# Two accumulator halves of each output: one reduction on VectorE in place of a ScalarE copy and a VectorE add

## The chip, the cores and the metric

The kernel runs on one core of one Trainium2 chip. The metric is the device time of one execution in microseconds (us).

## The reference, cut to what matters

The program is a two-block network on one sequence of T = 256 rows of width D = 2048, all in fp32. The first block has an even layer (gated short convolution, a state-space mixer `ssd` with 4 groups, memory attention) and an odd layer (latent attention `mla` with 16 heads, memory attention); the second has a retention mixer (8 heads) and a squared-ReLU MLP of width 8192. What matters here is that nearly all of the work is matrix products of the 256 rows with weights that are used once:

```python
proj = h @ w_in                                   # 2048 -> some 9000 columns, even layer
q  = (rms_norm(c_q,  mla_q_norm_w)  @ mla_w_uq)   # odd layer, rank 768
kv = (rms_norm(c_kv, mla_kv_norm_w) @ mla_w_ukv)  # odd layer, rank 512
return x + jnp.concatenate([y_a, y_b, y_m], axis=-1) @ w_out
...
def squared_relu_mlp(h, w_up, w_down):
    return jnp.square(jax.nn.relu(h @ w_up)) @ w_down
```

and that each product's result is then scaled, gated, added to the residual, or fed to an attention.

## The kernel before, in words

**Products in three parts.** fp32 factors are split in two parts each, hi and lo, of the type that TensorE takes at its full rate (`F32R`): w = w_hi + w_lo, h = h_hi + h_lo. A product is w_hi·h_hi + w_hi·h_lo + w_lo·h_hi. The activations lie transposed, as tiles of 128 features by T = 256 positions, hi and lo side by side (`hs`, `ys`, `lat`: 512 columns). A "panel" is the weights of 128 output features: 16 tiles of 128x128 as a rule, 6 or 8 in parts of the mla stage. For each tile, line 1821 multiplies w_hi with the 512 columns [h_hi, h_lo] into one accumulator bank of 512 columns, and line 1827 multiplies w_lo with the 256 columns of h_hi into the bank's first 256 columns. So at the end the bank `pj[:, k]` holds the output in two halves, columns 0 to 255 and 256 to 511, and the output is their sum. There are two such banks (`NB = 2`), used in turn.

**Panels by rows.** The value projections and the MLP's down projection are computed the other way round (`row_panel`, lines 1851 to 1855): all three parts go to the same 512 columns, and nothing is left to add. The change does not touch how these are taken from the bank.

**Splitting the weights.** The weights arrive by SyncE's queue in `raw` (4 panels deep). For each half of a panel, ScalarE writes `w_hi` (a copy that rounds, line 508), and VectorE writes `w_lo = raw - w_hi` (line 947). `w_hi` and `w_lo` hold two panels, so the split of panel p + 2 waits until TensorE has begun to use the half behind it in panel p (`half_started`), and TensorE waits for `split_ready`, VectorE's last word on a half.

**Taking an output.** `copy_half` on ScalarE (lines 510 to 513) waits for `output_ready` from TensorE and copies the bank's first half to the buffer `half`; `evac` on VectorE (lines 949 to 960) waits for `half_copied`, adds the bank's second half to `half`, and signals `evacuated`. With `scale` it then multiplies the sum by a row of factors (line 960). TensorE opens output o + 2 in the same bank only after output o is evacuated. 371 outputs go this way.

**The order of the work.** Each engine's program is written out by hand. In one panel step the engines do, with smaller pieces of the stage between:

```python
split(name, i, j, 0)        # ScalarE: w_hi of the first half of panel j + 2
copy_half(name, i, j)       # ScalarE
split(name, i, j, 1)
...
split(name, i, j, 0)        # VectorE: w_lo of the same halves
evac(name, i, j, dst)       # VectorE
split(name, i, j, 1)
```

ScalarE's second split of a step has no wait of its own for the buffer: it relies on the wait for `output_ready` that stands ahead of it.

**The two places to follow.** In the mla stage (8 passes, `mla_body`, 8 panel steps each) steps 0 to 2 make two query outputs and the rotary one (output 2), step 3 makes outputs 3 and 4 from one panel: output 4 takes the bank that output 2 had. Output 2 goes to `qr`, which GpSimd turns (line 469) before VectorE adds the turned part (lines 1564 and 1566) and TensorE multiplies for the scores (line 2173). In the ssd stage (4 passes, `ssd_body`, 12 panels of 16 tiles each) the last two steps hold the state-space tail: VectorE's lines 1338 to 1342, then 1325 to 1333 (the sum of squares), one small product on TensorE at tile 15 of panel 11 (line 2076), the variance (line 984), ScalarE's rsqrt by Ln and Exp (lines 523 to 527, with a load of the activation table), then output 11, VectorE's Newton step (lines 971 to 977), the gated memory output and the scaled outputs (line 1358 and 1363). The stage out0 behind it starts from those.

Of the kernel before, what the change touches and what calls it, by code (L numbers as in the profile page):

```python
# [25 lines left out]
P = 128  # L26
T = 256
# [95 lines left out]
def build(nc, streams, w_dt, vecs, consts, mla_mask, ret_tab, ret_decay, pos, x, mem, out):  # L123
    ctx = ExitStack()
    with ctx:
# [14 lines left out]
        kv = sb("kv", [P, 2048])  # L140
        half = sb("half", [P, NB, T])
        wdt = sb("wdt", [P, 16, 32])
# [88 lines left out]
        output_ready = sem("output_ready")  # L231
        half_copied = sem("half_copied")
        evacuated = sem("evacuated")
# [261 lines left out]
        def _(act):  # L495
# [13 lines left out]

            def copy_half(name, i, o, weight=1):  # L510
                c = outputs(name, i)
                act.wait_ge(output_ready, c(o, 1))
                A(half[:, c.slot(o, NB)], pj[:, c.slot(o, NB), 0:T], ACT.Copy).then_inc(half_copied, weight)  # L513

            def rows_out(name, i, r, dst, scale=1.0, sums=None):
                O = outputs(name, i)
                act.wait_ge(output_ready, O(4 + r, 1))
                A(dst, pj[:, O.slot(4 + r, NB)], ACT.Copy, scale=scale, accum_out=sums).then_inc(half_copied, 1)
                act.drain().then_inc(evacuated, 1)
# [43 lines left out]
            def mem_body(i):  # L563
                for j in range(8):
                    split("mem", i, j, 0)
                    if j < 4:
                        copy_half("mem", i, j)
                    if j == 7:
# [27 lines left out]
            def gate_body(i):  # L596
                for j in range(4):
                    if j == 1:
                        act.wait_ge(evacuated, outputs("gate", i)(0, 1 + NB))
                        A(th_g, z_g, ACT.Tanh, scale=0.5).then_inc(S["gate_tanh"], 1)  # L600
                    split("gate", i, j, 0)
                    copy_half("gate", i, j)
                    split("gate", i, j, 1)
# [6 lines left out]
            def gate_out_body(i):  # L610
                for j in range(4):
                    if i == 1 and j == 2:
                        act.wait_ge(S["dte_logits"], 1)
                        A(cum_out, mx[0:64, 2, 0:128], ACT.Copy).then_inc(S["cum_ready"], 1)
                        A(cum, mx[:, 1, 64:128], ACT.Copy)
                        A(dte, mx[:, 1, 0:32], ACT.Exp).then_inc(S["dte_ready"], 1)
                    copy_half("gate_out", i, 2 * j)
# [6 lines left out]
                    copy_half("gate_out", i, 2 * j + 1)  # L624
                    split("gate_out", i, j, 1)
# [3 lines left out]
            def residual(name, ppo):  # L629
# [3 lines left out]
                def body(i):  # L633
                    for j in range(len(SHAPES[name][0])):
                        split(name, i, j, 0)
                        if j % ppo == ppo - 1:
                            o = j // ppo
                            copy_half(name, i, o)
                        split(name, i, j, 1)
# [25 lines left out]
            def ssd_body(i):  # L665
                O = outputs("ssd", i)
                M = Count(0, 1, i)
                for j in range(12):
# [66 lines left out]
            def latent_q():  # L735
                for j in range(6):
# [6 lines left out]
                    if j == 0:  # L743
                        rsqrt(NORM["b_latent"] + 1, nv, ny)
                    copy_half("latent_q", 0, j)
                    split("latent_q", 0, j, 1)
# [6 lines left out]
            def latent_kv():  # L753
                for j in range(5):
                    if j == 4:
                        lat_squares(4, kvsq, 0, 4)
                    split("latent_kv", 0, j, 0)
                    if j == 1:
                        mem_turned(0)
                    copy_half("latent_kv", 0, j)  # L760
# [14 lines left out]
            def memq_body(i):  # L775
                name = f"memq{i}"
                M = Count(4, 2, i)
                for j in range(4):
# [12 lines left out]
                    copy_half(name, 0, j)  # L791
                    split(name, 0, j, 1)
# [14 lines left out]
            def mla_body(i, opening=False):  # L807
                O = outputs("mla", i)
                for j in range(8):
# [11 lines left out]
                    if j == 3:  # L821
                        copy_half("mla", i, 3)
                    split("mla", i, j, 0)
                    if j == 3:
                        copy_half("mla", i, 4)
                    if j < 3:
                        copy_half("mla", i, j)
                    if j == 4:
                        act.wait_ge(output_ready, O(5, 1))
                        A(vrow_, pj[:, O.slot(5, NB)], ACT.Copy).then_inc(half_copied, 1)  # L830
                        act.drain().then_inc(evacuated, 1)
                    if j == 5:
                        copy_half("mla", i, 6)
                    if j == 7:
                        act.wait_ge(S["mla_pt"], i * 1 + 1)
                        A(pt_.rearrange("p (u c) -> p u c", u=2), mx[:, 3:5, 0:384],
                          ACT.Copy).then_inc(S["mla_pt_copied"], 1)
                        copy_half("mla", i, 7)
                    split("mla", i, j, 1)
# [6 lines left out]
            def ret_body(name, first):  # L846
                def body(i, opening=False):
                    O = outputs(name, i)
                    for j in range(12):
# [16 lines left out]
                        if j < 4 or j >= 8:  # L866
                            copy_half(name, i, j if j < 4 else j - 2)
                        if j == 7:
# [18 lines left out]
            for b in range(FF_BLOCKS):  # L887
                def up_body(i, opening=False):
                    for j in range(4):
                        split(f"up{b}", i, j, 0)  # L890
                        copy_half(f"up{b}", i, j)
                        split(f"up{b}", i, j, 1)
# [6 lines left out]
                def down_body(i):  # L899
                    name = f"down{b}"  # L900
                    for j in range(4):
# [3 lines left out]
                        if j == 3:  # L905
                            act.wait_ge(output_ready, outputs(name, i)(1, 1))
                            act.nop().then_inc(half_copied, 2)
                        split(name, i, j, 1)
# [27 lines left out]
        def _(dve):  # L936
# [671 lines left out]
            def ret_body(name, first):  # L1608
                def body(i, opening=False):
# [30 lines left out]
                    for j in range(12):  # L1640
# [817 lines left out]
```

## Time and profile before

| | |
|---|---|
| median of 3 runs | 2695.31 us (2694.66 to 2696.9) |
| the profiled execution | 2695.13 us, span of its instructions 2693.6 us |
| TensorE products (PE) | busy 2659.9 us, 99% of the span |
| TensorE weight loads (PEld) | 2291.9 us, 85% |
| VectorE (DVE) | 1889.4 us, 70% |
| ScalarE (ACT) | 1395.7 us, 52% |
| GpSimd (POOL) | 61.4 us, 2% |
| transfers | 502.20 MB, 186 GB/s |
| granted TensorE clock | full in every slice but the last |

The profile is of one execution. A group's row gives the line, the engine, what is written from what, the count, the busy time, the mean of one in ns, and behind the last bar the idle time of that engine just ahead of these instructions with what ended it. PE rows tell of multiplications, PEld rows of weight loads, which run ahead of them. Ends of multiplications are modelled, so a gap in PE is best read from starts.

### The profile page before, as it was taken

Reading aid. Unit: us, or ns where it says so; the run is one execution under the profiler, and the core shown is the slowest. Engines: PE = TensorE matmul, PEld = TensorE weight load, DVE = VectorE, ACT = ScalarE, POOL = GpSimd, SP = SyncE. Lnnn points to the kernel's source line nnn. Section 1 sums busy time; section 2 is a strip of 40 time slices with the busy share of each in tenths; the row PEclk is TensorE's granted clock in tenths of the full one; section 3 lists DMA queues with packets and bytes.
Section 4 is the critical chain, followed back from the end, with each engine's and each line's share of the span. In section 5 each row is a group of like instructions: output and inputs, shape, how many; then the busy total and the mean of one; then the engine's idle time right before and its main releaser. Section 6 shows DMA issues by size and latency. Waiting matters only on the chain.

```text
span 2693.6 us, 42729 instructions
## 1 busy us (share of the span) xinstructions
PE 2659.9 (99%) x14622; PEld 2291.9 (85%) x14622; DVE 1889.4 (70%) x2945; ACT 1395.7 (52%) x2090; POOL 61.4 (2%) x84
## 2 busy tenths in 40 slices
PE   8999999999999999999999999999999999999998
PEld 7888888888888888888888888888888888888886
DVE  6766678888777777776777656666776576575674
ACT  5554467665555555565555545554554343444443
POOL 0000000000000111000000000000000000000000
PEclk9999999999999999999999999999999999999999
DMA  7755565555673454666555555555555656556553
GB/s 272 208 202 187 187 209 191 180 186 174 193 245 129 151 156 141 201 194 211 177 186 177 176 189 173 181 179 173 201 178 198 198 186 193 189 187 199 190 187 125
DMA packets 120007, 502.20 MB, mean 186 GB/s; under 512 B 9168, under 2 KB 9296, under 8 KB 82160
## 3 DMA queue, kind: packets, MB, share of 16 engines
q1 hardware_dynamic: 115456, 480.28, 53.4%
q0 software_dynamic: 4032, 20.03, 2.2%
q8 instruction: 54, 0.88, 0.1%
q10 hardware_dynamic: 432, 0.74, 0.1%
q14 instruction: 33, 0.27, 0.0%
HBM read 492.58 MB, written 8.43 MB: 186 GB/s over the span
## 4 chain that ended last, share of the span: by engine, by line
PE 85%; issue 7%; DVE 3%; ACT 2%; DVEq 1%; POOL 1%; DMA 0%; ACTq 0%; SPq 0%; POOLq 0%
PE pj L1821 39%; PE pj L1827 19%; PE pj L1851 7%; PE pj L1855 7%; PE pj L1854 7%; DVE w_lo L947 1%; ACT w_hi L508 1%; POOL gen L469 1%; PE pj L2279 1%; PE mx L1869 1%; PE mx L2237 1%; PE pj L2004 1%; PE pj L2282 0%; PE mx L2255 0%; DMA xT<-in_mem 0%
## 5 line engine op out<-in xcount | busy, mean ns | idle before, releaser
L947 DVE TENSOR_TENSOR w_lo<-raw,w_hi 128x1024 fp32r<-128x1024 f32 (+1 forms) x1010 | 1130.6, 1126 | 487.8 <-ACT w_hi L508 477.4
L508 ACT ACTIVATE w_hi<-raw 128x1024 fp32r<-128x1024 f32 (+1 forms) x1010 | 981.8, 977 | 719.7 <-PE pj L1821 377.8
L1821 PE MATMUL pj<-hs,w_hi 128*128 128x512 f32 x3792 | 1205.9, 399 | 0.6 <-DVE w_lo L947 0.6
L1827 PEld LDWEIGHTS pj<-hs,w_lo 128*128 128x128 f32 x3792 | 712.3, 188 | 167.9
L1827 PE MATMUL pj<-hs,w_lo 128*128 128x256 f32 x3792 | 745.8, 278 | 0.0
L1821 PEld LDWEIGHTS pj<-hs,w_hi 128*128 128x128 f32 x3792 | 581.4, 189 | 5.9 <-issue 1.9
L1821 PE MATMUL pj<-ys,w_hi 128*128 128x512 f32 x1328 | 418.2, 396 | 5.4 <-DVE ys L967 3.8
L513 ACT ACTIVATE half<-pj 128x256 f32<-128x256 f32 x371 | 140.8, 379 | 385.7 <-PE pj L1827 364.5
L1827 PEld LDWEIGHTS pj<-ys,w_lo 128*128 128x128 f32 x1328 | 249.5, 188 | 58.8
L1827 PE MATMUL pj<-ys,w_lo 128*128 128x256 f32 x1328 | 261.1, 278 | 0.0
L1851 PE MATMUL pj<-w_hi,ys 128*128 128x512 f32 x576 | 224.6, 390 | 0.0
L1854 PE MATMUL pj<-w_lo,ys 128*128 128x512 f32 x576 | 224.2, 389 | 0.0
L1855 PE MATMUL pj<-w_hi,ys 128*128 128x512 f32 x576 | 224.1, 389 | 0.0
L1821 PEld LDWEIGHTS pj<-ys,w_hi 128*128 128x128 f32 x1328 | 202.4, 189 | 7.3 <-DVE ys L967 4.4
L955 DVE TENSOR_TENSOR gen<-pj,half 128x256 f32<-128x256 f32 x228 | 95.8, 420 | 61.5 <-ACT half L513 59.8
L1855 PEld LDWEIGHTS pj<-w_hi,ys 128*128 128x128 f32 x576 | 108.1, 188 | 22.5
L1851 PEld LDWEIGHTS pj<-w_hi,ys 128*128 128x128 f32 x576 | 108.1, 188 | 22.3
L1854 PEld LDWEIGHTS pj<-w_lo,ys 128*128 128x128 f32 x576 | 108.2, 188 | 22.2
L1851 PE MATMUL pj<-w_hi,hs 128*128 128x512 f32 x256 | 100.5, 393 | 0.0
L1855 PE MATMUL pj<-w_hi,hs 128*128 128x512 f32 x256 | 99.7, 390 | 0.0
L1854 PE MATMUL pj<-w_lo,hs 128*128 128x512 f32 x256 | 99.7, 390 | 0.0
L1821 PE MATMUL pj<-lat,w_hi 128*128 128x512 f32 x208 | 68.7, 407 | 2.6 <-DVE gen L960 1.5
(346 smaller groups left out, 2002.4 us busy)
## 6 DMA issues: line engine op xcount, KB each, us to landing
raw<-in_w_up SPq DMA_DIRECT2D x64, 1024.0 KB, 4.9
raw<-in_w_down SPq DMA_DIRECT2D x64, 1024.0 KB, 5.7
raw<-in_w_ssd SPq DMA_DIRECT2D x48, 1024.0 KB, 4.8
raw<-in_w_ret_a SPq DMA_DIRECT2D x48, 1024.0 KB, 4.8
raw<-in_w_ret_b SPq DMA_DIRECT2D x48, 1024.0 KB, 4.9
raw<-in_w_out SPq DMA_DIRECT2D x64, 640.0 KB, 3.9
raw<-in_w_gate SPq DMA_DIRECT2D x32, 1024.0 KB, 4.9
raw<-in_w_mem SPq DMA_DIRECT2D x16, 1024.0 KB, 7.3
```

The lines of the kernel that those rows point to most:

```text
L469: ins = nc.gpsimd.tensor_tensor(qro[a:a + 32], qr[b:b + 32], sinT[b:b + 32], ALU.mult)
L508: A(hi, w, ACT.Copy).then_inc(hi_ready, 1)
L513: A(half[:, c.slot(o, NB)], pj[:, c.slot(o, NB), 0:T], ACT.Copy).then_inc(half_copied, weight)
L947: TT(lo, w, hi.bitcast(F32), ALU.subtract).then_inc(split_ready, 1)
L955: TT(dst, pj[:, k, T:2 * T], half[:, k], ALU.add).then_inc(evacuated, weight)
L1821: ins = mm(pj[:, k], w_hi[:, s + g, u], moving[t], start=opens and t == 0, stop=False)
L1827: ins = mm(pj[:, k, 0:T], w_lo[:, s + g, u], moving[t][:, 0], start=False, stop=closes and t == order[-1])
L1851: ins = mm(bank, x_hi, hi, start=opens and u == 0, stop=False)
L1854: mm(bank, x_hi, lo, start=False, stop=False)
L1855: ins = mm(bank, x_lo, hi, start=False, stop=closes and u == 3)
L1869: return nc.tensor.transpose(dst, src, ident)
L2004: ins = mm(pj[:, k], w_hi[:, s + h, u], src[:, t], start=t == 0, stop=False)
```

## The change

ScalarE no longer copies the half, and the buffer `half` and the semaphore `half_copied` are gone. ScalarE keeps the wait for `output_ready` at the same place (`panel_done`), since its next split relies on it. VectorE's `evac` now waits for `output_ready` and takes the sum with one reduction over a view of the whole bank, in which the two halves are the inner axis: for each of 256 columns it reads column t and column t + 256.

```diff
-        half = sb("half", [P, NB, T])
...
-            def copy_half(name, i, o, weight=1):
+            def panel_done(name, i, o):
                 c = outputs(name, i)
                 act.wait_ge(output_ready, c(o, 1))
-                A(half[:, c.slot(o, NB)], pj[:, c.slot(o, NB), 0:T], ACT.Copy).then_inc(half_copied, weight)
...
-                A(dst, pj[:, O.slot(4 + r, NB)], ACT.Copy, scale=scale, accum_out=sums).then_inc(half_copied, 1)
+                A(dst, pj[:, O.slot(4 + r, NB)], ACT.Copy, scale=scale, accum_out=sums)
                 act.drain().then_inc(evacuated, 1)
...
-                    copy_half("ssd", i, j)
                     if j == 11:
                         nc.scalar.preload_act_table_set(EXP_TANH)
+                    panel_done("ssd", i, j)
+                    if j == 11:
                         act.wait_ge(evacuated, O(11, 1 + NB))
...
             def evac(name, i, o, dst, weight=1, scale=None, via=None):
...
-                dve.wait_ge(half_copied, c(o, 1))
+                dve.wait_ge(output_ready, c(o, 1))
                 k = c.slot(o, NB)
                 if scale is None:
-                    TT(dst, pj[:, k, T:2 * T], half[:, k], ALU.add).then_inc(evacuated, weight)
+                    v.reduce_sum(dst, pj[:, k].rearrange("p (q t) -> p t q", q=2), AX.X).then_inc(evacuated, weight)
                 else:
                     via = dst if via is None else via
-                    TT(via, pj[:, k, T:2 * T], half[:, k], ALU.add)
+                    v.reduce_sum(via, pj[:, k].rearrange("p (q t) -> p t q", q=2), AX.X)
                     dve.drain()
                     TT(dst, via, scale, ALU.mult).then_inc(evacuated, weight)
...
-                            dve.wait_ge(half_copied, outputs(name, i)(5, 1))
+                            dve.wait_ge(evacuated, outputs(name, i)(5, 1 + NB))
```

All other calls of `copy_half` become calls of `panel_done` at the same place. In the instructions as built, TensorE, GpSimd and SyncE have the same rows as before.

ScalarE in the last panel step of the ssd stage, before (`half` is the removed buffer, `gen` scratch; what a row waits for stands in brackets):

```order
L508 ACTIVATE w_hi<-raw 128x1024 [waits half_started]
L523 ACT_TABLE_LOAD
L525 ACTIVATE gen<-gen 128x256 [waits var_ready]
L527 ACTIVATE gen<-gen 128x256
L513 ACTIVATE half<-pj 128x256 [waits output_ready]
L715 ACT_TABLE_LOAD
L716 REGISTER_ALU
L717 ACTIVATE gen<-gen 128x256 [waits evacuated]
L508 ACTIVATE w_hi<-raw 128x1024 [waits weights_loaded1]
```

and ScalarE at the same place now (the changed file's lines stand 2 to 3 lower):

```order
L506 ACTIVATE w_hi<-raw 128x1024 [waits half_started]
L520 ACT_TABLE_LOAD
L522 ACTIVATE gen<-gen 128x256 [waits var_ready]
L524 ACTIVATE gen<-gen 128x256
L711 ACT_TABLE_LOAD
L714 REGISTER_ALU [waits output_ready]
L715 ACTIVATE gen<-gen 128x256 [waits evacuated]
L506 ACTIVATE w_hi<-raw 128x1024 [waits weights_loaded1]
```

The copy is gone, the table load stands ahead of the wait for the output, and VectorE's step for this output no longer stands behind ScalarE's rsqrt.

VectorE in steps 1 to 3 of a pass of the mla stage, before:

```order
L955 TENSOR_TENSOR gen<-pj,half 128x256 [waits half_copied]
L945 REGISTER_ALU
L947 TENSOR_TENSOR w_lo<-raw,w_hi 128x512 [waits weights_hi_ready]
L945 REGISTER_ALU
L947 TENSOR_TENSOR w_lo<-raw,w_hi 128x512 [waits weights_hi_ready]
L952 REGISTER_ALU
L955 TENSOR_TENSOR gen<-pj,half 128x256 [waits half_copied]
```

and VectorE at the same place now:

```order
L952 TENSOR_REDUCE gen<-pj 128x256 [waits output_ready]
L942 REGISTER_ALU
L944 TENSOR_TENSOR w_lo<-raw,w_hi 128x512 [waits weights_hi_ready]
L942 REGISTER_ALU
L944 TENSOR_TENSOR w_lo<-raw,w_hi 128x512 [waits weights_hi_ready]
L949 REGISTER_ALU
L952 TENSOR_REDUCE gen<-pj 128x256 [waits output_ready]
```

Nothing changes its place: the add of output 1 and of output 2 are replaced where they stood, each by a reduction.

## Rows read from the trace of the kernel before

**Rows 1.** The page's first part: span, then busy time (share) xinstructions by engine.

```profile
span 2693.6 us, 42729 instructions
PE 2659.9 (99%) x14622; PEld 2291.9 (85%) x14622; DVE 1889.4 (70%) x2945; ACT 1395.7 (52%) x2090; POOL 61.4 (2%) x84
```

**Rows 2.** The page's costliest groups: the copy of a half, and the add.

```profile
L513 ACT ACTIVATE half<-pj 128x256 f32<-128x256 f32 x371 | 140.8, 379 | 385.7 <-PE pj L1827 364.5
...
L955 DVE TENSOR_TENSOR gen<-pj,half 128x256 f32<-128x256 f32 x228 | 95.8, 420 | 61.5 <-ACT half L513 59.8
```

**Rows 3.** Single lines: VectorE's reductions; duration in ns min/median/max.

```profile
L1224 DVE TENSOR_REDUCE small<-mx x8: 681/683/685, 363.3 to 869.9; 128x2 f32<-128x512 f32 x8
```

```profile
L1540 DVE TENSOR_REDUCE small<-kv x8: 419/419/422, 895.1 to 1101.4; 128x2 f32<-128x256 f32 x8
```

**Rows 4.** Waits of PE and PEld: who for whom, us in total, times, longest.

```profile
PE pj L1821 <- DVE ys L967: 3.8, 2, 2.7
PE pj L1821 <- DVE gen L960: 1.5, 1, 1.5
...
PE mx L2116 <- DVEq L1444: 0.9, 1, 0.9
PE mx L2033 <- DVE xT L960: 0.9, 1, 0.9
PE pj L1821 <- DVE lat L1462: 0.8, 1, 0.8
...
PE pj L1821 <- DVE xT L960: 0.4, 1, 0.4
```

```profile
PEld pj L1821 <- DVE gen L955: 1.6, 7, 0.2
```

**Rows 5.** Timeline of one mla pass: start us, us, engine line, [idle before].

```profile
943.58 0.69 DVE L947 TENSOR_TENSOR w_lo<-raw,w_hi 128x512 fp32r<-128x512 f32 x1 [0.86 <-ACT w_hi L508]
944.19 0.41 DVE L955 TENSOR_TENSOR gen<-pj,half 128x256 f32<-128x256 f32 x1
944.52 1.28 DVE L947 TENSOR_TENSOR w_lo<-raw,w_hi 128x512 fp32r<-128x512 f32 x2
945.73 0.41 DVE L955 TENSOR_TENSOR gen<-pj,half 128x256 f32<-128x256 f32 x1
```

```profile
946.27 0.72 PE L1821 MATMUL pj<-lat,w_hi 128*128 128x512 f32 x2
```

```profile
946.22 4.38 POOL L469 TENSOR_TENSOR gen<-gen 32x256 f32<-32x256 f32 x4 [24.30 <-DVE gen L955]
```

**Rows 6.** Timeline at the end of the first ssd pass: VectorE, ScalarE, PE.

```profile
410.81 0.42 DVE L955 TENSOR_TENSOR gen<-pj,half 128x256 f32<-128x256 f32 x1
...
414.18 0.42 DVE L1333 TENSOR_TENSOR xT<-xT 128x256 f32<-128x256 f32 x1
...
417.43 0.42 DVE L955 TENSOR_TENSOR gen<-pj,half 128x256 f32<-128x256 f32 x1 [1.24 <-ACT half L513]
```

```profile
416.71 0.42 ACT L527 ACTIVATE gen<-gen 128x256 f32<-128x256 f32 x1
417.03 0.37 ACT L513 ACTIVATE half<-pj 128x256 f32<-128x256 f32 x1
```

```profile
414.65 0.70 PE L2076 MATMUL mx<-xT,con 128*128 128x256 f32 x2
...
415.42 0.40 PE L1827 MATMUL pj<-hs,w_lo 128*128 128x256 f32 x2
...
424.39 0.74 PE L1821 MATMUL pj<-hs,w_hi 128*128 128x512 f32 x2 [0.20 <-DVE w_lo L947]
```

**Rows 7.** One window of the ssd stage: busy us (x) of each engine.

```profile
404.00:471.40 67.40, 67.20 (x392) 58.65 (x391) 55.92 (x99) 47.95 (x87) 1.79 (x4) 1.00 0.55 190
```

**Rows 8.** Timeline of VectorE: an add behind other work, a split behind ScalarE.

```profile
910.56 0.42 DVE L958 TENSOR_TENSOR gen<-pj,half 128x256 f32<-128x256 f32 x1
```

```profile
289.87 1.22 DVE L947 TENSOR_TENSOR w_lo<-raw,w_hi 128x1024 fp32r<-128x1024 f32 x1 [0.50 <-ACT w_hi L508]
```

More of the change, by code:

```diff
@@ L231, in build @@
         output_ready = sem("output_ready")
-        half_copied = sem("half_copied")
         evacuated = sem("evacuated")
@@ L566, in mem_body @@
                     if j < 4:
-                        copy_half("mem", i, j)
+                        panel_done("mem", i, j)
                     if j == 7:
@@ L601, in gate_body @@
                     split("gate", i, j, 0)
-                    copy_half("gate", i, j)
+                    panel_done("gate", i, j)
                     split("gate", i, j, 1)
@@ L616, in gate_out_body @@
                         A(dte, mx[:, 1, 0:32], ACT.Exp).then_inc(S["dte_ready"], 1)
-                    copy_half("gate_out", i, 2 * j)
+                    panel_done("gate_out", i, 2 * j)
                     split("gate_out", i, j, 0)
@@ L623, in gate_out_body @@
                         act.drain().then_inc(S["dt_exp"], 1)
-                    copy_half("gate_out", i, 2 * j + 1)
+                    panel_done("gate_out", i, 2 * j + 1)
                     split("gate_out", i, j, 1)
@@ L637, in body @@
                             o = j // ppo
-                            copy_half(name, i, o)
+                            panel_done(name, i, o)
                         split(name, i, j, 1)
@@ L744, in latent_q @@
                         rsqrt(NORM["b_latent"] + 1, nv, ny)
-                    copy_half("latent_q", 0, j)
+                    panel_done("latent_q", 0, j)
                     split("latent_q", 0, j, 1)
@@ L759, in latent_kv @@
                         mem_turned(0)
-                    copy_half("latent_kv", 0, j)
+                    panel_done("latent_kv", 0, j)
                     split("latent_kv", 0, j, 1)
@@ L790, in memq_body @@
                         lat_squares(3, qsq[1], 8, 2)
-                    copy_half(name, 0, j)
+                    panel_done(name, 0, j)
                     split(name, 0, j, 1)
@@ L821, in mla_body @@
                     if j == 3:
-                        copy_half("mla", i, 3)
+                        panel_done("mla", i, 3)
                     split("mla", i, j, 0)
                     if j == 3:
-                        copy_half("mla", i, 4)
+                        panel_done("mla", i, 4)
                     if j < 3:
-                        copy_half("mla", i, j)
+                        panel_done("mla", i, j)
                     if j == 4:
                         act.wait_ge(output_ready, O(5, 1))
-                        A(vrow_, pj[:, O.slot(5, NB)], ACT.Copy).then_inc(half_copied, 1)
+                        A(vrow_, pj[:, O.slot(5, NB)], ACT.Copy)
                         act.drain().then_inc(evacuated, 1)
                     if j == 5:
-                        copy_half("mla", i, 6)
+                        panel_done("mla", i, 6)
                     if j == 7:
@@ L837, in mla_body @@
                           ACT.Copy).then_inc(S["mla_pt_copied"], 1)
-                        copy_half("mla", i, 7)
+                        panel_done("mla", i, 7)
                     split("mla", i, j, 1)
@@ L866, in body @@
                         if j < 4 or j >= 8:
-                            copy_half(name, i, j if j < 4 else j - 2)
+                            panel_done(name, i, j if j < 4 else j - 2)
                         if j == 7:
@@ L890, in up_body @@
                         split(f"up{b}", i, j, 0)
-                        copy_half(f"up{b}", i, j)
+                        panel_done(f"up{b}", i, j)
                         split(f"up{b}", i, j, 1)
@@ L906, in down_body @@
                             act.wait_ge(output_ready, outputs(name, i)(1, 1))
-                            act.nop().then_inc(half_copied, 2)
                         split(name, i, j, 1)
```

## The prediction

> **What bounds the kernel now.** I read the page's busy times first: TensorE is busy for 2659.9 us of a span of 2693.6 us [rows 1], so no engine but TensorE matters for long, and the most that better hand-overs could give back is what TensorE idles. The reader should take from this that VectorE at 1889.4 us and ScalarE at 1395.7 us [rows 1] have time to spare on average, and that the average is not the question: what counts is where TensorE waits, and for whom. So the waits of TensorE are the second view [rows 4]. They are few: the longest are at the exits of stages, where the next stage's input is made by a serial chain on VectorE, and there are a few inside the latent and memory-query steps. One is regular, though too small for the PE list: in 7 of the 8 mla passes the weight load of line 1821 waits some 0.2 us for VectorE's add, line 955 [rows 4]. The third view is the groups: 371 copies of a half at 379 ns each on ScalarE, and the adds at 420 ns on VectorE [rows 2].
>
> The profiled execution took 2695.13 us, 1.5 us more than its span, and 0.2 us less than the median of the three runs, 2695.31. The sum below is made against the profiled execution, and the 0.2 us is added at the end.
>
> **What the change removes and adds.** It removes 371 x 379 ns = 141 us of ScalarE work. ScalarE's wait for the output stays where it was, so ScalarE gets no further ahead; its next `w_hi` starts about 0.3 us sooner after an output. It turns 371 adds on VectorE into reductions. What one costs has to be bounded, since no row shows a reduction with a hop between its two operands. The nearest rows are VectorE's reduction of 512 elements from the accumulator, 683 ns, and of 256 elements, 419 ns [rows 3]: 1.03 ns per element and 157 ns fixed. The new reduction reads 512 elements, so I take 683 ns, from the row with the same count, the same memory and the same operation. The low end is 420 ns, if it went at one output per step as the add does [rows 2]. The high end is 157 + 512 x 2.06 = 1210 ns, if each hop of 256 columns costs a second step. At 683 ns one output costs VectorE 0.26 us more, 98 us in all: from 1889 to 1987 us, 74% of the span. From "output ready" to "sum there" the path was a copy and an add, 0.38 + 0.42 = 0.80 us, and becomes 0.68 us, if VectorE is free.
>
> I do not count that 0.12 us 371 times. TensorE has two banks and comes back to one only after a whole panel, so it gains or loses only at the places in [rows 4]. I go through them.
>
> **The mla passes, the largest term.** VectorE is released by ScalarE at 943.58, and from there works without a pause: split, add of output 1, two splits, add of output 2 from 945.73 to 946.14 [rows 5]. TensorE needs output 2's bank for output 4 and starts at 946.27, just after that add [rows 5]. Two of the adds stand in this run of work, both before the release, and neither waits for ScalarE's copy, so the shorter path gains nothing here. TensorE gets the bank 2 x 0.26 = 0.53 us later. GpSimd's turn starts with the same add [rows 5], so the next wait (VectorE's lines 1564 and 1566, then the scores) moves by the same amount and does not take it back. 7 passes: +3.7 us. The opening pass has a wait for line 1462 in front (0.8 us, [rows 4]) that has one add in its run, and a second add behind it: +0.5 us.
>
> **Latent and memory-query steps.** Three waits have one add in an unbroken run of VectorE's work ahead of them: line 2116 for VectorE at line 1444, line 1821 for `gen` L960 and for `xT` L960 [rows 4]; an example is the add at 910.56 ahead of the 1.5 us wait [rows 8]. Each +0.26 us: +0.8 us. The wait of line 2033 (0.9 us, [rows 4]) has both: its run begins at a `w_hi` that stands behind a copy, about 0.3 us sooner now, and has one add: 0.
>
> **Splits behind a copy.** At the exit of the gate stage VectorE's last split waits 0.50 us for ScalarE's `w_hi` [rows 8], which stood right behind a copy. It gets it 0.2 to 0.3 us sooner, less what the longer reduction takes ahead of it. There is one more such place in the memory-query steps. I take -0.25 us each: -0.5 us.
>
> **The ssd stage.** VectorE runs without a pause from before the add at 410.81 to line 1333 at 414.18, and TensorE's small product at 414.65 waits for it [rows 6]: +0.26 us in each pass. Then the other way: output 11 was ready when the two products from 415.42 had ended, by about 415.9 [rows 6], but its copy stood behind ScalarE's Exp at 416.71 and was made at 417.03, so the add came at 417.43, after 1.24 us of idle time on VectorE [rows 6]. Now the reduction runs in that idle time, and the Newton step waits for the Exp alone. It starts at 417.43 + 0.34 = 417.77 before, and now, with everything 0.26 us later, at 417.13 + 0.26 + 0.06 = 417.45: 0.32 us sooner. The split that the next pass waits for at 424.39 (0.20 us, [rows 6]) comes that much sooner, and the wait is gone, most of it used up by the 0.26 us. Net -0.1 us in three passes; in the last, whose chain ends in the 2.7 us wait for `ys` L967 [rows 4], -0.3 us. Together -0.6 us.
>
> **What is hidden, and by what.** All other reductions lie beside TensorE's panel of 16 tiles. A window of the ssd stage, the fullest, has VectorE busy for 55.92 of 67.40 us [rows 7], 11.5 us idle for 12 outputs; the reductions take 3.2 us of that. If that cover were gone, each output would cost TensorE up to 0.26 us. The removed 141 us of ScalarE were idle cover already, and are worth nothing by themselves. The wait on `evacuated` in place of `half_copied` in the retention stage stands ahead of a split that ends the same chain as before: 0.
>
> **Sum:** 3.7 + 0.5 + 0.8 - 0.5 - 0.6 = +3.9 us. 2695.31 + 3.9 = 2699.2 us, which is 0.14% more. A measurement of this kernel can tell about 0.2%, 5.4 us, from no change, so the forecast is "no change", a little on the slow side.
>
> **Rivals.**
> A, slower: **the hop costs.** If VectorE reads single words 1 KB apart at a lower rate, the reduction takes up to 1210 ns, and every term grows. By the high end the mla passes cost 2 x 0.79 us in each of 8, 12.6 us in place of 4.2. With 2.4 for the three latent waits, 0.5 at line 2033, 0 for the two splits and +1.7 in ssd this gives +17 us, 2712.5 us. Halfway, at 950 ns, it is about +10 us, 2705.5 us. It decides above some 750 ns, where the sum passes 5.4 us. For it: no row shows such a view. Against it: the add read one operand from the accumulator and one from elsewhere at the rate of one pair per step, so a step's fixed price does not depend on where the next word lies. Chance 0.22.
> The Trainium skill, "Vector Engine (DVE) Microarchitecture Reference", section "Measured stream behaviour on trn2", says that a source port that hops on every element takes 1.73 ns per column where a contiguous one takes 1.054; by that the reduction would be an estimated 157 + 512 x 1.73 = 1040 ns, and the result would lie between the two figures of this rival. The same section says that a one-source operation whose reads alternate between two regions and which writes one word for two read ran at the full rate, which is this case's shape; both are told of the other memory, and no row here shows either.
>
> B, slightly faster or equal: **the adds hide, the hand-over shows.** If TensorE has more slack at 946.27 than the 0.2 us weight-load wait suggests, the mla and latent terms vanish, and what remains is -0.5 and -0.6: 2694.2 us. For it: the PE list does not show the mla wait at all. Against: start and release lie 0.13 us apart [rows 5]. A gain over 0.2% would need a third of all that TensorE waits. Chance 0.14.
>
> C, slower: **backlog in ssd.** If VectorE's idle time in ssd lies only where it waits for TensorE, and the steps with the convolutions have none, the 12 outputs of a pass cost 0.26 us each in 4 passes: +12.5 on top of 3.9, 2712 us at most; half of it, 2706 us, is likelier. Against: [rows 7]. Chance 0.10.
>
> That the change would not do what it says has nothing for it: the rows as built show no `half` left, and TensorE's order is the same.
>
> **Chances.** My forecast has 0.54, A 0.22, B 0.14, C 0.10. The forecast's own spread is some 2.5 us either way (2696.5 to 2702), so a tenth or so of it passes the 5.4 us line at 2700.7. Slower by over 0.2%: A and C nearly whole, and 0.08 of the forecast, 0.39. Faster by over 0.2%: a part of B, 0.04. Within 0.2%: 0.57. The range that should hold the time 8 times in 10 goes from B's end with a little room, 2693.5, to 2711, which leaves out A's and C's far ends.
>
> **What would show each step right or wrong.** The group of reductions: 371 of them at 683 ns, VectorE's busy time at some 1987 us, ScalarE's at 1255. The mla passes: 28.7 us apart before (GpSimd's 24.30 us of idle time and 4.38 us of work, [rows 5]), 29.2 after, and PEld waits for the reduction near 0.7 us in place of 0.2. The end of an ssd pass: the reduction of output 11 ahead of the Exp's end, the wait at the next pass's first split gone. A reduction above 750 ns, or new waits of TensorE for `w_lo` inside ssd, would make the prediction wrong on the slow side; mla passes of unchanged length would make it wrong on the fast side.

## The result and the profile after

| | before | after |
|---|---|---|
| median of 10 runs each | 2695.40 us | 2702.85 us |
| lowest to highest | 2694.36 to 2696.90 | 2701.92 to 2703.37 |
| profiled execution (span) | 2695.13 (2693.6) | 2702.06 (2700.5) |

The changed kernel takes 1.0027 times as long, 95% interval 1.0019 to 1.0035: 7.45 us more. That is inside the forecast range (2693.5 to 2711.0) and on its slow side, but 3.7 us over the forecast, and over the 0.2% (5.4 us) that I had put between "no change" and "slower", where I had 0.39. It is also above the forecast's own spread (2696.5 to 2702): the range holds it because it was drawn wide for the rivals A and C, and neither of these came true.

The page's first part after the change, as [rows 1]:

```profile
span 2700.5 us, 42702 instructions
PE 2663.5 (99%) x14622; PEld 2293.8 (85%) x14622; DVE 1980.5 (73%) x2945; ACT 1295.5 (48%) x1719; POOL 61.4 (2%) x84
```

The groups of VectorE that answer to the add of [rows 2], and the largest that waits for TensorE (busy us, mean ns, then idle time before them and its releasers):

```profile
L952 DVE TENSOR_REDUCE gen<-pj 128x256 f32<-128x512 f32 x228 | 156.5, 686 | 21.6 <-PE pj L1824 18.6 <-PE pj L2006 2.4
L952 DVE TENSOR_REDUCE kv<-pj 128x256 f32<-128x512 f32 x72 | 49.7, 691 | 5.7 <-PE pj L1824 3.5 <-PE pj L2279 0.8
...
L955 DVE TENSOR_REDUCE gen<-pj 128x256 f32<-128x512 f32 x59 | 40.5, 686 | 27.8 <-PE pj L1824 27.6
```

The waits of PE and of PEld after, as [rows 4] (lines stand 2 to 3 lower):

```profile
PE pj L1818 <- DVE gen L952: 3.1, 16, 0.2
PE pj L1818 <- DVE ys L964: 3.0, 2, 2.1
PE pj L1818 <- DVE gen L957: 2.0, 2, 1.7
...
PE mx L2113 <- DVEq L1441: 1.2, 1, 1.2
PE pj L1818 <- DVE lat L1459: 1.0, 1, 1.0
PE mx L2073 <- DVE xT L1330: 0.9, 4, 0.2
```

```profile
PEld pj L1818 <- DVE gen L952: 4.1, 9, 0.5
```

Three things are to be seen. The reduction takes 686 ns, so it is not the hop that made the kernel slower. TensorE now waits for the reduction itself, line 952, in 16 places where its list of waits had none. And the wait for `w_lo` that [rows 6] show in ssd is gone from the list, as is 0.8 us of the wait for `ys`: there are gains too, and the result is a difference of the two.

To see where, I matched the same TensorE instructions of both traces one by one, in order, and subtracted their start times ("the matched starts" below). The shift grows in steps. One mla pass shows how; PE's timeline before and after, the instruction ahead of each step and the one behind it:

```profile
942.24 0.39 PE L1827 MATMUL pj<-lat,w_lo 128*128 128x256 f32 x2
942.47 0.64 PE L1821 MATMUL pj<-lat,w_hi 128*128 128x512 f32 x2
...
944.48 0.28 PE L1827 MATMUL pj<-lat,w_lo 128*128 128x256 f32 x1
944.66 0.73 PE L1821 MATMUL pj<-lat,w_hi 128*128 128x512 f32 x2
...
945.94 0.39 PE L1827 MATMUL pj<-lat,w_lo 128*128 128x256 f32 x2
```

```profile
943.94 0.39 PE L1824 MATMUL pj<-lat,w_lo 128*128 128x256 f32 x2
944.38 0.70 PE L1818 MATMUL pj<-lat,w_hi 128*128 128x512 f32 x2
...
946.44 0.28 PE L1824 MATMUL pj<-lat,w_lo 128*128 128x256 f32 x1
946.90 0.73 PE L1818 MATMUL pj<-lat,w_hi 128*128 128x512 f32 x2 [0.17 <-DVE gen L952]
...
948.18 0.39 PE L1824 MATMUL pj<-lat,w_lo 128*128 128x256 f32 x2
948.78 0.72 PE L1818 MATMUL pj<-lat,w_hi 128*128 128x512 f32 x2 [0.21 <-DVE gen L952]
```

The shift is 1.70 us at the first row, 1.96 at 944.48, 2.24 at 945.94, and 2.51 at the start that stood at 946.27 before [rows 5]. That is three steps of 0.27 us in this pass, each where TensorE comes back to a bank that VectorE has just emptied. The prediction had two.

The shift added up by stages, in us, from the profiled executions (stages by their time before), beside what the prediction had for them. The last three columns are experiments told of below:

| stage | predicted | changed kernel | no copy, short add | copy kept, reduction | mix |
|---|---|---|---|---|---|
| gate exit, to 300 | -0.25 | -0.3 | -0.3 | 0.0 | -0.2 |
| gate_out, to 404 | 0 | **+1.1** | 0.0 | +1.7 | 0.0 |
| ssd and its exit, to 760 | -0.6 | -0.5 | -2.1 | +2.9 | -2.1 |
| line 2028 at 763 | 0 | +0.3 | 0.0 | +0.3 | 0.0 |
| memory-query and latent, to 860 | 0 | -0.2 | -0.5 | +0.3 | -0.4 |
| latent and opening mla pass, to 905 | +0.8 | +1.1 | -0.3 | +1.3 | 0.0 |
| mla passes, to 1125 | +4.0 | +4.7 | -1.0 | +5.9 | -1.2 |
| out1 and its end, to 1290 | 0 | **+0.9** | -0.3 | +1.2 | 0.0 |
| opening retention pass, to 1310 | 0 | **+0.5** | 0.0 | +0.6 | 0.0 |
| sum, from 60 us to the end | +3.9 | +7.6 | -4.5 | +14.7 | -3.8 |

The sums are over all instructions from 60 us on, so they hold a little that no row does: with copy and reduction, +0.55 us behind 1310.

The first 20 us are left out of it: there the start shifts by -0.9 to +0.6 us from kernel to kernel, also in kernels that change nothing before 880 us, as the first loads land.

### The profile page after: what moved, and what is told of

Its sections match the earlier page's. It is cut to its first block, busy times and chain, and to the rows that moved or that the text cites. A ratio compares the mean times of both kernels' runs of the same rounds, so it can differ in the third digit from the quotient of the medians.

```text
span 2700.5 us, 42702 instructions
## 1 busy us (share of the span) xinstructions
PE 2663.5 (99%) x14622; PEld 2293.8 (85%) x14622; DVE 1980.5 (73%) x2945; ACT 1295.5 (48%) x1719; POOL 61.4 (2%) x84
## 4 chain that ended last, share of the span: by engine, by line
PE 85%; issue 7%; DVE 3%; ACT 2%; DVEq 1%; POOL 1%; DMA 0%; ACTq 0%; SPq 0%; POOLq 0%
PE pj L1818 39%; PE pj L1824 19%; PE pj L1848 7%; PE pj L1852 7%; PE pj L1851 7%; ACT w_hi L506 1%; DVE w_lo L944 1%; POOL gen L467 1%; PE pj L2276 1%; PE mx L1866 1%; PE mx L2234 1%; PE pj L2001 1%; PE pj L2279 0%; PE mx L2252 0%; DMA xT<-in_mem 0%
## 5 line engine op out<-in xcount | busy, mean ns | idle before, releaser
L944 DVE TENSOR_TENSOR w_lo<-raw,w_hi 128x1024 fp32r<-128x1024 f32 (+1 forms) x1010 | 1129.9, 1125 | 468.4 <-ACT w_hi L506 458.8
L952 DVE TENSOR_REDUCE gen<-pj 128x256 f32<-128x512 f32 x228 | 156.5, 686 | 21.6 <-PE pj L1824 18.6
L955 DVE TENSOR_REDUCE gen<-pj 128x256 f32<-128x512 f32 x59 | 40.5, 686 | 27.8 <-PE pj L1824 27.6
```

Source lines behind the costliest of these rows:

```text
L944: TT(lo, w, hi.bitcast(F32), ALU.subtract).then_inc(split_ready, 1)
L952: v.reduce_sum(dst, pj[:, k].rearrange("p (q t) -> p t q", q=2), AX.X).then_inc(evacuated, weight)
L955: v.reduce_sum(via, pj[:, k].rearrange("p (q t) -> p t q", q=2), AX.X)
```

## The experiments

The theory, T: a longer operation on VectorE costs 0.26 us wherever TensorE waits behind VectorE's own run of work; the copy gave back time only where it stood ahead of work on ScalarE that somebody waits for; the two add up place by place. The rivals were a loss that is spread over all outputs (S), a loss that comes from ScalarE's changed order (P), gains that are noise (N), and the hop. Where an output is to keep the old hand-over, the kernels have a test on the stage's name and the output's number:

```diff
             def copy_half(name, i, o, weight=1):
                 c = outputs(name, i)
                 act.wait_ge(output_ready, c(o, 1))
+                if reduced(name, o):
+                    act.nop().then_inc(half_copied, weight)
+                    return
                 A(half[:, c.slot(o, NB)], pj[:, c.slot(o, NB), 0:T], ACT.Copy).then_inc(half_copied, weight)
...
             def evac(name, i, o, dst, weight=1, scale=None, via=None):
                 c = outputs(name, i)
+                if reduced(name, o):
+                    dve.wait_ge(output_ready, c(o, 1))
+                    k = c.slot(o, NB)
+                    two = pj[:, k].rearrange("p (q t) -> p t q", q=2)
...
```

and below each is given by what `reduced` returns.

**The reduction everywhere but in mla.** `return name != "mla"`.

> The changed kernel, but the outputs of the mla stage keep the old hand-over (ScalarE's copy, VectorE's add); all other outputs have the reduction. Theory T (what costs is 0.26 us more of VectorE per output at the places where TensorE waits behind VectorE; three such steps of 0.265 us in each of 7 mla passes, less 0.165 us by which ScalarE's Exps come sooner): the mla stage's 4.4 us are gone, 2702.85 - 4.4 = 2698.4 us, and the mla passes are 28.7 us apart again. Rival S (the loss is spread evenly over the 371 outputs, for instance by contention at the accumulator): 64 of 371 outputs change back, 7.45 x 64 / 371 = 1.3 us, so 2701.6 us.

Measured 2697.56 us (2696.68 to 2698.26), 5.3 us under the changed kernel. **The reduction in mla alone.** `return name == "mla"`.

> The kernel before, with the reduction in the mla stage alone (there ScalarE only waits for the output and copies nothing). Theory T: +4.4 us, 2695.4 + 4.4 = 2699.8 us, the mla passes 29.3 us apart, everything else as before. Rival S (spread evenly over the outputs): +1.3 us, 2696.7 us.

Measured 2700.48 us (2699.63 to 2700.95), 5.4 us over the kernel before, ratio 1.0018 [1.0009, 1.0027]. GpSimd works once per mla pass, so its timeline gives the length of a pass: idle time and four operations. First the changed kernel, then the reduction everywhere but in mla, then in mla alone:

```profile
1007.36 4.37 POOL L467 TENSOR_TENSOR gen<-gen 32x256 f32<-32x256 f32 x4 [24.93 <-DVE gen L952]
```

```profile
1003.75 4.38 POOL L473 TENSOR_TENSOR gen<-gen 32x256 f32<-32x256 f32 x4 [24.31 <-DVE gen L977]
```

```profile
1007.19 4.38 POOL L473 TENSOR_TENSOR gen<-gen 32x256 f32<-32x256 f32 x4 [24.93 <-DVE gen L967]
```

29.30, 28.69 and 29.31 us: with the old hand-over the pass is as long as in [rows 5], and with the reduction 0.62 us longer. 56 outputs of 371 (7 of a pass's 8 have a copy; my 64 above was one per pass too many) carry 5.4 of 7.45 us. Rival S, with 1.3 us, falls; the matched starts say the same, since in the changed kernel the shift stays within 0.02 us over 58 us inside an ssd pass (430 to 488), where the reductions go on all the time. T's 4.4 us was too small by 1 us, and the matched starts say why: it had left out the opening pass (+0.8 us at 880 to 885) and a step at 911.62.

**The add's old length without the copy.**

```diff
-                    v.reduce_sum(dst, pj[:, k].rearrange("p (q t) -> p t q", q=2), AX.X).then_inc(evacuated, weight)
+                    TT(dst, pj[:, k, T:2 * T], con[:, 0:T], ALU.add).then_inc(evacuated, weight)
```

and the same in the branch with a scale.

> The changed kernel, but VectorE's operation reads only the second half from the accumulator and adds a constant of equal shape from SBUF (so the first half of each output is left out, and the outputs' values are others): the add's old form and old duration, about 420 ns, with no copy on ScalarE. Theory T: the steps of +0.26 us vanish and the gains remain, which the aligned traces put at -4.2 us in all (start, exits of stages, Newton step of ssd, Exps of mla): 2691.2 us. Rival N (the removed copy is worth nothing and the small negative steps are noise): 2695.4 us. Rival P (the loss has nothing to do with VectorE's time, but comes from the changed order on ScalarE): near 2702.85 us.

Measured 2690.21 us (2690.02 to 2691.30), ratio 0.9982 [0.9973, 0.9991]. **Copy kept and waited for, reduction in place of the add.**

```diff
-                    TT(dst, pj[:, k, T:2 * T], half[:, k], ALU.add).then_inc(evacuated, weight)
+                    v.reduce_sum(dst, pj[:, k].rearrange("p (q t) -> p t q", q=2), AX.X).then_inc(evacuated, weight)
```

> The kernel before, with ScalarE's copy kept and waited for, and the reduction of both halves in place of the add. Theory T: all the steps of +0.26 us of the changed kernel, none of its gains: 7.45 + 4.2 = 11.7 us over the kernel before, 2707 us. Rival P (the loss comes from the copy's removal and the changed order on ScalarE, not from VectorE's time): 2695.4 us, as before. The reductions take 684 ns as in the changed kernel.

Measured 2710.31 us (2709.96 to 2711.12), ratio 1.0054 [1.0040, 1.0068]. The groups of the two, in this order:

```profile
L952 DVE TENSOR_TENSOR gen<-pj,con 128x256 f32<-128x256 f32 x228 | 95.9, 420 | 26.5 <-PE pj L1824 22.1 <-PE pj L2006 3.9
```

```profile
L955 DVE TENSOR_REDUCE gen<-pj 128x256 f32<-128x512 f32 x228 | 156.6, 687 | 52.8 <-ACT half L513 51.4
```

These two kernels take the change apart. The copy's removal, with the table load moved ahead of the wait, is worth 4.9 us; the loss comes with VectorE's longer operation, 0.27 us each, since P would have given 2702.85 and 2695.4. From "no copy" to the changed kernel only VectorE's operation differs (420 or 686 ns; it also reads 512 words of the bank in place of 256, and the flat shift inside ssd shows that this alone costs TensorE nothing), and that costs 12.6 us; from "before" to "copy kept", 15.2 us. T had 11.7 us for the second. The table shows the largest missing part: in ssd +2.9 us in place of 1.6 (the changed kernel's -0.5 without the gain of 2.1). There copy and reduction stand in one chain behind ScalarE's Exp, and TensorE's waits at 424.39 and 427.30 grow by 0.25 and 0.28 us over the kernel before, in each of three passes; in the changed kernel the gain at 424.39 covered this. Smaller parts are 0.6 us more in gate_out and three steps behind 1310 us (+0.55 together, at 1514.56, 1521.63 and 1895.87), which the changed kernel does not have; I have no cause for these.

**Neighbouring words in place of words 1 KB apart.**

```diff
-                    v.reduce_sum(dst, pj[:, k].rearrange("p (q t) -> p t q", q=2), AX.X).then_inc(evacuated, weight)
+                    v.reduce_sum(dst, pj[:, k].rearrange("p (t q) -> p t q", q=2), AX.X).then_inc(evacuated, weight)
```

and the same in the branch with a scale.

> The changed kernel, but the reduction adds neighbouring words (columns 2t and 2t+1) in place of words 1 KB apart, so each output's halves are not added (the sum of the halves is left out, neighbours are added in its place). If the hop between the two halves costs VectorE nothing (what the 684 ns of the changed kernel suggest): a reduction of 684 ns and the time of the changed kernel, 2702.85 us. Rival (part of the 684 ns is the hop, and 683 ns of the other reductions is chance): shorter reductions here, and up to the kernel of the old add's length, 2695 us or less.

Measured 2702.36 us (2701.91 to 2703.13), and the group:

```profile
L952 DVE TENSOR_REDUCE gen<-pj 128x256 f32<-128x512 f32 x228 | 156.5, 686 | 21.6 <-PE pj L1824 18.6 <-PE pj L2006 2.4
```

The same row as in the changed kernel, to the digit, and the same time. The hop costs nothing here.

**The reduction for output 0 of the mla passes alone.** `return name == "mla" and o == 0`.

> The kernel before, with the reduction (and no copy) for output 0 of an mla pass alone, one output in 371 x 8 / 371 passes, 8 in all. Theory T (TensorE comes back to output 0's bank for output 2 and waits for VectorE there too, a wait that the prediction did not count): +0.265 us in each of 8 passes, +2.1 us, 2697.3 us. The prediction's own account (only the adds of outputs 1 and 2 lie on the way to a wait): 0, 2695.2 us.

Measured 2697.14 us (2696.43 to 2698.96), 2.2 us over the kernel before; its ratio, 1.0008 [0.9999, 1.0017], does not exclude 1, but the pass does:

```profile
1004.79 4.37 POOL L473 TENSOR_TENSOR gen<-gen 32x256 f32<-32x256 f32 x4 [24.56 <-DVE gen L977]
```

28.93 us, 0.25 more than in [rows 5], for one output that the prediction had counted as hidden. The matched starts have the step of 0.27 us at 942.47 in each of the six later passes, and nowhere else in them; the two passes ahead of these have it at 880.06 and 914.04. The second of them has another +0.4 us at 921.96, where TensorE waits 0.48 us for VectorE's add; the changed kernel has no step there, and its cause is open. So the eight steps come to 2.2 us by the matched starts, and that the difference of the medians is 2.2 us as well is in part chance.

**The reduction in gate_out and out1 alone.** `return name in ("gate_out", "out1")`.

> The kernel before, with the reduction (and no copy) in the two residual stages gate_out and out1 alone, which the prediction held to be hidden. Theory T (VectorE's run of work between two outputs fills its time there, so each longer output reaches TensorE in part): +1.1 us in gate_out and +0.9 us in out1, 2695.2 + 2.0 = 2697.2 us. Rival H (the steps seen there in the changed kernel come from somewhere else, the reductions there are hidden): 2695.2 us.

Measured 2697.66 us (2696.77 to 2698.10), +2.7 us, ratio 1.0010 [1.0001, 1.0019]. Rival H falls. Matched starts: +1.1 us in gate_out, +1.0 in out1 and +0.27 at its end (line 2025 in the kernel before, at 1228). For gate_out the mechanism is on VectorE's timeline, before, and then in the changed kernel:

```profile
313.64 0.42 DVE L955 TENSOR_TENSOR gen<-pj,half 128x256 f32<-128x256 f32 x1
314.16 0.43 DVE L1211 TENSOR_TENSOR xT<-xT,gen 128x256 f32<-128x256 f32 x1
314.51 1.22 DVE L947 TENSOR_TENSOR w_lo<-raw,w_hi 128x1024 fp32r<-128x1024 f32 x1
315.64 0.82 DVE L1134 SCALAR_TENSOR_TENSOR gen<-gen 128x64 f32<-128x64 f32 x3
316.53 0.42 DVE L955 TENSOR_TENSOR gen<-pj,half 128x256 f32<-128x256 f32 x1
```

```profile
312.79 0.69 DVE L952 TENSOR_REDUCE gen<-pj 128x256 f32<-128x512 f32 x1
313.57 0.42 DVE L1208 TENSOR_TENSOR xT<-xT,gen 128x256 f32<-128x256 f32 x1
313.92 1.22 DVE L944 TENSOR_TENSOR w_lo<-raw,w_hi 128x1024 fp32r<-128x1024 f32 x1
315.05 0.82 DVE L1131 SCALAR_TENSOR_TENSOR gen<-gen 128x64 f32<-128x64 f32 x3
315.94 0.69 DVE L952 TENSOR_REDUCE gen<-pj 128x256 f32<-128x512 f32 x1
```

For some 14 us, five outputs, VectorE has no pause to speak of between two outputs, before or after: 2.89 us per output before, 3.15 after. TensorE brought an output every 2.79 us there (its outputs began at 314.50, 317.29, 320.08 and 322.87). While VectorE was only just slower, TensorE's two banks absorbed it. In the changed kernel TensorE takes VectorE's pace, and its outputs begin 3.06 and 3.19 us apart:

```profile
316.78 0.70 PE L1818 MATMUL pj<-ys,w_hi 128*128 128x512 f32 x2 [0.20 <-DVE gen L952]
...
319.84 0.73 PE L1818 MATMUL pj<-ys,w_hi 128*128 128x512 f32 x2
...
323.03 0.70 PE L1818 MATMUL pj<-ys,w_hi 128*128 128x512 f32 x2
```

That is 0.3 to 0.4 us with each of three outputs. In out1 it is not this: VectorE waits there for ScalarE at most outputs, 0.65 us and another 0.6 to 0.9 us, and the steps are of 0.1 us. The run shows that the reductions of the two stages cause them, not by which chain.

**The reduction for output 11 of the ssd passes alone.** `return name == "ssd" and o == 11`, with the preload of the table ahead of the wait, as in the change.

> The kernel before, with the reduction (and no copy, and the table preload ahead of the wait, as in the change) for output 11 of the ssd passes alone. Theory T: TensorE's first waits of the next pass vanish, -0.46 us in each of three passes, and the last pass's exit comes 0.6 us sooner: 2695.0 - 2.0 = 2693.0 us. The prediction's account of this piece alone, without its +0.26 us for output 10: 0.32 us of lead, of which the 0.2 us wait of three passes goes, and 0.3 us at the last: -0.9 us, 2694.1 us. Rival N: 2695.0 us.

Measured 2693.09 us (2692.15 to 2694.01), -1.8 us; the matched starts give -2.1. The ratio, 0.9993 [0.9984, 1.0002], does not tell it from 1, but TensorE's steps do: -0.46 to -0.48 us at the start of each of three passes, and -0.6 at the exit. (The prediction's own account, as that text gives it, is too small: without the +0.26 us of output 10 its lead is 417.77 - 417.19 = 0.58 us, so 3 x 0.20 + 0.58 = 1.2 us, 2693.8 us. The exit is as this account has it; the three passes, 0.47 in place of 0.20 us each, are not.) The same place as [rows 6] in this kernel, VectorE, then PE where the next pass begins:

```profile
415.44 0.42 DVE L1006 TENSOR_SCALAR gen<-mx 128x256 f32<-128x256 f32 x1
415.77 0.68 DVE L967 TENSOR_REDUCE gen<-pj 128x256 f32<-128x512 f32 x1
416.83 0.43 DVE L993 TENSOR_TENSOR gen<-gen 128x256 f32<-128x256 f32 x1 [0.37 <-ACT gen L534]
```

```profile
423.69 0.62 PE L1843 MATMUL pj<-hs,w_hi 128*128 128x512 f32 x2
...
424.39 0.63 PE L1843 MATMUL pj<-hs,w_hi 128*128 128x512 f32 x2
```

The reduction runs ahead of the Exp's end, in what was idle time, and the wait of [rows 6] is gone. Its price is worth a look. The view calls it 0.20 us. But PE's timeline of the kernel before reads

```profile
423.33 0.63 PE L1821 MATMUL pj<-hs,w_hi 128*128 128x512 f32 x2
...
425.21 0.63 PE L1821 MATMUL pj<-hs,w_hi 128*128 128x512 f32 x2
```

with the start at 424.39 of [rows 6] between them: 1.06 us and 0.82 us where this row otherwise comes every 0.70. The wait cost 0.48 us, in that the pair that begins with it was slow as well (0.74 us in place of 0.63).

**The mix.** The reduction only where the matched starts showed gains and no losses:

```diff
+def reduced(name, o):
+    return name in ("mem", "gate", "memq0") or (name, o) in (("ssd", 11), ("mla", 6))
```

> The kernel before, with the reduction (and no copy) only where the aligned traces show a gain and no loss: all outputs of the memory, gate and first memory-query steps, output 11 of an ssd pass (with the table preload moved ahead of it, as in the change) and output 6 of an mla pass; the other outputs keep copy and add. Theory T (gains sit where ScalarE's copy stands ahead of something that VectorE or TensorE waits for, losses where VectorE's own chain is waited for, and the two add up): -0.4 (start) - 0.3 (gate exit) - 2.0 (ssd) - 0.5 (first memory-query step) - 1.0 (Exps of the mla passes) = -4.2 us against the kernel before, 2691.0 us, faster than both. Rival N (the small negative steps are noise or belong to the run of the changed kernel as a whole): 2695.1 us, as before.

Measured **2691.59 us** (2690.42 to 2692.27), 3.4 us under the kernel before, ratio 0.9986 [0.9977, 0.9995], faster than both. The matched starts have -3.8 us. T's -4.2 had 0.4 us for the start in it, which is no gain but the spread of the first loads. The part of `("mla", 6)` is the plainest: the copy of output 6 stood ahead of ScalarE's Exps, which VectorE waits for (0.77 us before, 0.40 now), and the pass becomes 28.5 us long, some 0.2 less:

```profile
1000.71 4.37 POOL L473 TENSOR_TENSOR gen<-gen 32x256 f32<-32x256 f32 x4 [24.12 <-DVE gen L977]
```

## Why the prediction was right, and where it was wrong

**The reduction's price, right.** 683 ns taken from [rows 3], 686 to 691 measured. (The fixed part by these rows is 155 ns, not 157; nothing hangs on it.) VectorE's busy time came to 1980.5 us (1987 predicted). Rival A falls, by the changed kernel's rows and by the kernel with neighbouring words. By the Trainium skill, "Vector Engine (DVE) Microarchitecture Reference", section "Measured stream behaviour on trn2", a port that hops on every element would have made it some 1040 ns (an estimate from that page's figure, which is told of SBUF); no such price shows here, out of the accumulator. The same section's remark that a one-source operation that alternates between two regions, and writes one word for two read, went at the full rate is what this case's traces agree with, 686 ns with the hop and 686 without.

**ScalarE, a size off.** Predicted 1255 us busy, measured 1295.5 [rows 1: 1395.7]. 371 x 379 ns counted the copies by their own length, but they overlapped their neighbours: 100.2 us went, 0.27 us for a copy. ScalarE's timeline before shows it, a copy and the next split:

```profile
930.77 0.38 ACT L513 ACTIVATE half<-pj 128x256 f32<-128x256 f32 x1 [1.92 <-PE pj L1827]
931.05 0.62 ACT L508 ACTIVATE w_hi<-raw 128x512 fp32r<-128x512 f32 x1
```

This bore on no term of the sum.

**The mla passes, the mechanism right, one step missed, one gain missed.** The step "two of the adds stand in this run of work" looked back from one wait only. TensorE comes back to a bank for every output, and three of these returns find VectorE still at work: 7 x 3 x 0.267 = +5.6 us, not 3.7. Each return takes up its own 0.27 us, so none of them grows by two: PEld waits 0.50 us there, not 0.7. Against it stands a gain that I had called nothing by "the removed 141 us of ScalarE were idle cover already": the Exps of each pass come 0.165 us sooner, -1.2 us. Together +4.5 us. The opening pass had three such returns as well, +0.8 in place of +0.5.

**The three latent waits, right.** +0.27 us each at 850.86, 877.83 and 911.62 where I had 0.26, and 0 at line 2033. **The two splits behind a copy, right in place**: -0.27 at the gate's exit, -0.47 at 824.5 in place of -0.25.

**ssd, right by the sum only.** Predicted -0.6 us, measured -0.5. The lead of the Newton step was right: it starts 0.35 us sooner against the starts around it (0.32 predicted), with the 0.27 us of output 10 in it. The sum made from it was not. With the prediction's own figures each of three passes gains the wait of 0.20 us and loses 0.26 at output 10, which is +0.06 and not -0.1, and ssd comes to -0.1 us. The wait cost 0.48 us where I took it at its face, so output 11 gained 2.1 us (3 x 0.48 + 0.6) and not 1.2. Against it stand +0.27 us at output 10 in four passes and a loss that I had counted as hidden, +0.11 to +0.16 at 427.5 and its like in the next two passes. The trace of the changed kernel shows where this one comes from, VectorE, then PE:

```profile
426.60 0.69 DVE L952 TENSOR_REDUCE xT<-pj 128x256 f32<-128x512 f32 x1
```

```profile
427.33 0.74 PE L1818 MATMUL pj<-hs,w_hi 128*128 128x512 f32 x2
```

The reduction ends at 427.29, and TensorE's next panel begins right behind it with a slow pair, as at a return to a bank just emptied; the add before ended at 427.15, ahead of a start at 427.30. That -0.6 stood beside -0.5 was luck.

**"All other reductions lie beside TensorE's panel", wrong.** This is the step that failed. It argued from one stage's average, 11.5 us of VectorE idle in [rows 7], and from it to all stages. The runs of gate_out (+1.1 us), out1 (nine steps of some 0.1 us, 0.27 at its end, less a gain of 0.28 at 1285.94), line 2028 (+0.27) and the opening retention pass (+0.5) were never looked at. In ssd itself it held but for the one output a pass told of above: the changed kernel's list has no wait for `w_lo`, and rival C falls. Of these, gate_out and out1 were tried alone and bear it out; line 2028 and the retention pass were not tried by themselves, but both are absent with the short add and there again with copy and reduction. For the retention step the changed kernel's trace shows the wait, 0.28 us for VectorE's scaled output,

```profile
1303.24 0.73 PE L1818 MATMUL pj<-hs,w_hi 128*128 128x512 f32 x2 [0.28 <-DVE gen L957]
```

and two reductions in the chain ahead of it, at 1293.43 and at 1302.01, 2 x 0.27 us.

**Rival B, in part.** None of the losses that I had counted hid, but its other half, that the hand-over has gains of its own, was bigger than any case of mine: 4.9 us, some 40% of what VectorE's extra length costs (12.6 us).

So the sum was low by 3.7 us: 1.9 in the mla passes and 0.3 in the opening one, less 1.2 for the Exps; 2.8 in what was held to be hidden (1.1 + 0.3 + 0.9 + 0.5); -0.2 in the memory-query steps and +0.1 in ssd. Errors of both signs stand in it, so the sum was nearer than its parts.

## What to carry to other kernels

A fusion that takes work from an engine with time to spare, and lengthens an operation on the engine that the bottleneck waits for, is to be priced place by place, and from both sides: every return of TensorE to a bank is a place, not only those on the list of waits, and in each stage the first question is whether VectorE's work between two outputs is already as long as TensorE's (2.89 against 2.79 us in gate_out), not how busy it is on average. Out1 shows that this question alone does not find every place. Where both kinds of place exist, use each form where it wins: 56 of the 371 outputs with the reduction made a kernel that is faster than either. Two kernels that each carry one half of a change (the short operation without the copy, the long one with it) tell more than any single reading, since they also show the gains that the losses hide.

## What the runs showed of the hardware that I had not expected

- VectorE's reduction of two words 1 KB apart in the accumulator takes as long as one of neighbours, 686 ns for 256 sums.
- A wait of TensorE that the view gives as 0.20 us cost 0.48 us from start to start: the pair behind it took 0.74 in place of 0.63 us. PEld's row is nearer, 0.40 us for that wait; in the changed kernel's mla passes it shows 0.50 for the wait that PE's row gives as 0.17 and that cost 0.45 from start to start:

```profile
424.39 0.30 PEld L1821 LDWEIGHTS pj<-hs,w_hi 128*128 128x128 f32 x2 [0.40 <-DVE w_lo L947]
```

```profile
946.90 0.30 PEld L1818 LDWEIGHTS pj<-lat,w_hi 128*128 128x128 f32 x2 [0.50 <-DVE gen L952]
```

- Taking out an operation of 379 ns on ScalarE freed 0.27 us. By the Trainium skill, "ScalarE: Activation LUTs", section "What ACT_TABLE_LOAD costs", ScalarE's operations that stand back to back overlap by some 93 ns; the timeline's 0.10 us (379 ns long, the next 0.28 us behind) agrees.
